# Layer norms of a decoder layer without statistics instructions: row sums from the residual adds, squares summed by ScalarE

## The chip, the cores and the metric

The kernel runs on one core of one Trainium2 chip. The metric is the device time of one execution in microseconds (us), from launch to end. Three executions of the kernel before took 700.11, 701.52 and 701.88 us; the median is 701.52 us. A further execution was recorded by the hardware profiler; all rows below come from that one.

Engines: PE is TensorE (matmul; PEld its weight loads), DVE is VectorE, ACT is ScalarE, POOL is GpSimd, SP is the engine whose queue issues most DMAs. Each engine runs its own list of instructions strictly in order and waits on semaphores (`s_...`) that others raise.

## What is computed

A decoder layer over 512 tokens of width 1024: a projection, sparse attention and an mLSTM, an output projection, then two layer norms around a mixture of experts, and a gated per-layer embedding. The change touches the two layer norms only.

```
def _layer_norm(x, g, b):
    mu = jnp.mean(xf, axis=-1, keepdims=True)
    var = jnp.mean(jnp.square(xf - mu), axis=-1, keepdims=True)
    y = (xf - mu) * lax.rsqrt(var + LN_EPS)
    return (y * g + b)

    ...
    mix = jnp.concatenate([y_a, y_m], axis=-1) @ w_out
    x = _layer_norm(DEEPNORM_ALPHA * x + mix, ln1_g, ln1_b)
    ffn = _hierarchical_moe(x, rg_w, rg_b, re_w, re_b, e_gate, e_up, e_down)
    x = _layer_norm(DEEPNORM_ALPHA * x + ffn, ln2_g, ln2_b)
    return x + jax.nn.sigmoid(x @ ple_gate_w) * (p_i @ ple_proj_w)
```

## The kernel before

Tokens stand on the 128 partitions in four tiles t = 0 to 3 of 128 tokens by 1024 features; the tile being normed is `mine[:, t, :]` (the buffer `res`). All order is written out by hand, one list per engine. Every large matmul product is taken in three passes on a high and a low part of each operand (`three`, L1693 to L1695); ACT rounds the high part, DVE subtracts it to give the low part.

**First norm, ahead of the router.** PE multiplies out the output projection per tile and half (`token_major`). When a half is done (`s_wot`), DVE's `mixed` adds it to the scaled residual (`residual`, L1346), then reads the half again with a statistics instruction (`norm_stats`, L1350); after the second half it merges the statistics (L1356), adds epsilon (L1358), and raises `s_ve`. POOL takes the power -0.5 (`inverse`, L698, `s_rs`). Meanwhile DVE subtracts the mean and multiplies by the norm's weights in place (`norm_centre`, L1362) and then, once POOL is done, scales and adds the bias (`norm_scale`, L1369, `s_ln`). PE turns the tile (`turn_first`, L1922: eight 128x128 transposes), ACT copies the two halves as high parts (L941), DVE makes the low parts (`low_first`, L1375). `route(0)` multiplies tiles 0 and 1 with the router's weights, `route(1)` tiles 2 and 3. Everything after (choice of experts, gather, experts) waits for `route(1)`.

**Second norm, behind the experts.** For each tile DVE adds the two experts' rows, each times its gate, to the residual (`expert_sum`, L1654, twice 128x1024), takes the statistics (`expert_variance`: L1350 twice, L1356, L1358), centres and scales. PE turns the tile, ACT and DVE make high and low parts (L1002, L1375), and PE multiplies with the gate's weights (`gate`, four quarters of 12 matmuls per tile and half). Ahead of that PE works off five products of the per-layer embedding (`embed`, L1933), and ACT carries each from PSUM to SBUF (`ple_out`, L936). In ACT's list all five `ple_out` stand ahead of the first copy of a turned tile:

```
            for u in range(AHEAD, 2 * NT):
                ple_out(u)
            act.wait_ge(s_glo, 2)
            ...
            for t in range(NT):
                turned_high(2 * t)
                turned_high(2 * t + 1)
```

In PE's list too, the five `embed` stand ahead of the first turn. Between the turns of tiles 0 and 1, ACT also rounds the last quarter of the gate's weights (`round_gate(3)`, L972), and DVE splits it (`split_gate(3)`, L1614) before PE's `gate(0, 3)`.

The code around the change:

Of the kernel before, what the change touches and what calls it, by code (L numbers as in the profile page):

```python
# [6 lines left out]
BF16 = mybir.dt.bfloat16  # L7
I32 = mybir.dt.int32
ALU = mybir.AluOpType
ACT = mybir.ActivationFunctionType  # L10
# [4 lines left out]
SEQ, DM = 512, 1024  # L15
# [6 lines left out]
EPS = 1e-5  # L22
# [51 lines left out]
def hybrid_layer(nc, d, out, x1_dram, pair_dram):  # L74
    ctx = ExitStack()
    with ctx:
# [3 lines left out]
        def sem(name):  # L80
            return ctx.enter_context(nc.semaphore(name))
# [188 lines left out]
        stat8 = small[:, 0:48].rearrange("p (t c) -> p t c", t=NT)  # L270
        mv8 = small[:, 48:56].rearrange("p (t c) -> p t c", t=NT)
        rs8 = small[:, 56:60]
        ve8 = small[:, 60:64]
        gate_w = [small[:, 64:68], small[:, 68:72]]
# [62 lines left out]

        s_pair = [sem(f"s_pair{t}") for t in range(NT)]
        s_ghi, s_glo, s_gt = sem("s_ghi"), sem("s_glo"), sem("s_gt")
        s_r2, s_bn2, s_ve2, s_rs2, s_ln2 = [sem(n) for n in ("s_r2", "s_bn2", "s_ve2", "s_rs2", "s_ln2")]  # L340
        s_x2t, s_x2hi, s_x2lo = sem("s_x2t"), sem("s_x2hi"), sem("s_x2lo")
        s_sig, s_mix, s_out = sem("s_sig"), sem("s_mix"), sem("s_out")
# [406 lines left out]
        def _(act):  # L749
# [184 lines left out]
            def ple_out(u):  # L934
                act.wait_ge(s_pp, u + 1)
                a.activation(ple_parts[u], ple_bank[u][:, :], ACT.Copy).then_inc(s_pev, 1)  # L936

            for u in range(2 * NT):
                t, half = u // 2, u % 2
                act.wait_ge(s_x1t, u + 1)  # L940
                a.activation(a_hi[:, 4 * half:4 * half + 4, t * P:(t + 1) * P],  # L941
                             turned_1[u][:, :].rearrange("p (k c) -> p k c", k=4), ACT.Copy).then_inc(s_x1hi, 1)
                if u == 1:
                    act.wait_ge(s_wr, 16)
                    act.wait_ge(s_wo, 2)
                    a.activation(w_hi[:, WR_AT:3 * GW], wr_raw.rearrange("p k c -> p (k c)"), ACT.Copy)\
                        .then_inc(s_wrs, 1)
                if u == 5:
                    copy_logits(0)
            copy_logits(1)  # L950

# [72 lines left out]
        def _(dve):  # L1024
# [319 lines left out]
            def residual(t, half):  # L1344
                r = mine[:, t, half * 512:(half + 1) * 512]
                v.scalar_tensor_tensor(out=r, in0=r, scalar=ALPHA, in1=bank[4 * (1 - half) + t][:, :],  # L1346
                                       op0=ALU.mult, op1=ALU.add).then_inc(s_r, 1)

            def norm_stats(t, half, count):
                v.bn_stats(stat8[:, t, 6 * half:6 * half + 6], mine[:, t, half * 512:(half + 1) * 512])\  # L1350
                    .then_inc(count, 1)

            def norm_variance(t, count, base, done):

                dve.wait_ge(count, base)
                v.bn_aggr(mv8[:, t, :], stat8[:, t, :]).then_inc(count, 1)  # L1356
                dve.wait_ge(count, base + 1)
                v.tensor_scalar(ve8[:, t:t + 1], mv8[:, t, 1:2], EPS, None, ALU.add).then_inc(done, 1)  # L1358

            def norm_centre(t, done):  # L1360
                m = mine[:, t, :]
                v.scalar_tensor_tensor(out=m, in0=m, scalar=mv8[:, t, 0:1], in1=ln_g, op0=ALU.subtract,  # L1362
                                       op1=ALU.mult).then_inc(done, 1)

            def norm_scale(t, done, ready):
                m = mine[:, t, :]
                dve.wait_ge(done, 2 * t + 1)
                dve.wait_ge(ready, t + 1)
                v.scalar_tensor_tensor(out=m, in0=m, scalar=rs8[:, t:t + 1], in1=ln_b, op0=ALU.mult,  # L1369
                                       op1=ALU.add).then_inc(done, 1)  # L1370

            def turned_low(u, banks, hi, lo):
# [7 lines left out]
            def mixed(t, half):  # L1380
                dve.wait_ge(s_xn[t], 16)
                dve.wait_ge(s_wot, 2 * t + half + 1)
                residual(t, half)
                dve.wait_ge(s_r, 2 * t + half + 1)
                norm_stats(t, half, s_bn)
                if half:
                    norm_variance(t, s_bn, 3 * t + 2, s_ve)
# [12 lines left out]
            mixed(1, 1)  # L1400
            norm_centre(1, s_ln)
            norm_scale(1, s_ln, s_rs)
            low_first(0)
            dve.wait_ge(s_wrs, 1)
            v.tensor_tensor(w_lo[:, WR_AT:3 * GW], wr_raw.rearrange("p k c -> p (k c)"),
                            w_hi[:, WR_AT:3 * GW].bitcast(F32), ALU.subtract).then_inc(s_wrs, 1)
            mixed(2, 0)
            mixed(2, 1)
            norm_centre(2, s_ln)
            mixed(3, 0)  # L1410
            norm_scale(2, s_ln, s_rs)
            low_first(1)
            mixed(3, 1)
            norm_centre(3, s_ln)
            norm_scale(3, s_ln, s_rs)
            low_first(2)
            low_first(3)

            n = [0]
# [228 lines left out]
            def expert_sum(t, k):  # L1648
                if k == 0:
                    dve.wait_ge(s_pair[t], 16)  # L1650
                else:
                    dve.wait_ge(s_xn[t], 32)
                dve.wait_ge(s_r2, NT + 2 * t + k)
                v.scalar_tensor_tensor(out=mine[:, t, :], in0=pair_of(t)[:, k, :], scalar=gate_w[k][:, t:t + 1],  # L1654
                                       in1=mine[:, t, :], op0=ALU.mult, op1=ALU.add).then_inc(s_r2, 1)

            def expert_variance(t):
                dve.wait_ge(s_r2, NT + 2 * t + 2)
                for half in range(2):
                    norm_stats(t, half, s_bn2)  # L1660
                norm_variance(t, s_bn2, 3 * t + 2, s_ve2)


            for t in range(NT):
                expert_sum(t, 0)
                if t:
                    turned_low(2 * t - 2, turned_2, s_x2hi, s_x2lo)
                    turned_low(2 * t - 1, turned_2, s_x2hi, s_x2lo)
                expert_sum(t, 1)
                expert_variance(t)  # L1670
                if t == 0:
                    dve.wait_ge(s_lnw2, 32)
                norm_centre(t, s_ln2)
                norm_scale(t, s_ln2, s_rs2)
# [503 lines left out]
```

## Time and profile before

| | us |
|---|---|
| median of three executions | 701.52 (700.11 to 701.88) |
| the profiled execution, whole | 696.23 |
| its span, first to last instruction | 694.4 |
| mean granted TensorE clock over the span | 0.964 of full speed |
| PE busy | 640.6 (92%) |
| DVE busy | 366.9 (53%) |
| ACT busy | 179.0 (26%) |
| POOL busy | 162.4 (23%) |

A row of a timeline reads: start in us from the span's start, duration in us, engine, line of the code, operation, what it writes and reads with shapes, how many such, and in brackets how long the engine had stood idle before and what ended the wait. Line numbers are those of the kernel before; in the changed kernel the same functions stand some 10 lines further down.

### The profile page before, as it was taken

Reading aid. Unit: us, or ns where it says so; the run is one execution under the profiler, and the core shown is the slowest. Engines: PE = TensorE matmul, PEld = TensorE weight load, DVE = VectorE, ACT = ScalarE, POOL = GpSimd, SP = SyncE. Lnnn points to the kernel's source line nnn. Section 1 sums busy time; section 2 is a strip of 40 time slices with the busy share of each in tenths; the row PEclk is TensorE's granted clock in tenths of the full one; section 3 lists DMA queues with packets and bytes.
Section 4 is the critical chain, followed back from the end, with each engine's and each line's share of the span. In section 5 each row is a group of like instructions: output and inputs, shape, how many; then the busy total and the mean of one; then the engine's idle time right before and its main releaser. Section 6 shows DMA issues by size and latency. Waiting matters only on the chain.

```text
span 694.4 us, 10082 instructions
## 1 busy us (share of the span) xinstructions
PE 640.6 (92%) x3766; PEld 445.2 (64%) x3766; DVE 366.9 (53%) x849; ACT 179.0 (26%) x344; POOL 162.4 (23%) x173
## 2 busy tenths in 40 slices
PE   4989999999989999899957999899999999897997
PEld 3758797777767778788734555555555555543785
DVE  3379999677675648675964223122221122118956
ACT  5265224324322423340211111111111111115321
POOL 7305615001010000041203233233333323211100
PEclk9959999999999999999997999999999999998999
DMA  6502401401400040119986899999999999987003
GB/s 237 207 0 66 179 0 31 181 1 41 142 0 1 3 179 1 33 62 369 387 340 221 298 404 418 416 416 415 413 417 414 414 414 414 407 325 280 41 0 122
DMA packets 30502, 151.21 MB, mean 218 GB/s; under 512 B 7372, under 2 KB 7628, under 8 KB 16496
## 3 DMA queue, kind: packets, MB, share of 16 engines
q1 hardware_dynamic: 24048, 142.08, 51.7%
q0 software_dynamic: 6400, 8.42, 3.4%
q8 instruction: 32, 0.52, 0.3%
q14 instruction: 22, 0.18, 0.1%
HBM read 148.36 MB, written 14.68 MB: 235 GB/s over the span
## 4 chain that ended last, share of the span: by engine, by line
PE 62%; DVE 8%; DMA 7%; issue 3%; SPq 2%; ACT 1%; POOL 1%; DVEq 0%; POOLq 0%; ACTq 0%
PE bank L2012 16%; PE bank L2027 9%; PE bank L1693 8%; PE bank L1694 8%; PE bank L1695 8%; DMA slots<-in_w_exp_dram 4%; PE bank L1773 3%; SPq L488 2%; PE bank L2002 2%; PE bank L1782 2%; PE bank L1794 1%; PE bank L1823 1%; PE bank L2019 1%; PE bank L1814 1%; POOL small L698 1%
## 5 line engine op out<-in xcount | busy, mean ns | idle before, releaser
L1605 DVE COPY rows_x<-bank 128x128 f32<-128x128 f32 x40 | 11.7, 292 | 186.0 <-issue 100.7
L1693 PE MATMUL bank<-w_hi,a_hi 128*128 128x384 f32 (+1 forms) x240 | 89.7, 374 | 3.9 <-POOL w_lo L629 2.9
L1694 PE MATMUL bank<-w_lo,a_hi 128*128 128x384 f32 (+1 forms) x240 | 87.6, 365 | 0.0
L1695 PE MATMUL bank<-w_hi,a_lo 128*128 128x384 f32 (+1 forms) x240 | 87.6, 365 | 0.0
L1693 PE MATMUL bank<-a_hi,w_hi 128*128 128x512 f32 (+1 forms) x176 | 70.9, 403 | 11.5 <-POOL w_lo L622 9.9
L713 POOL DMA_INDIRECT pair_dram<-rows_x,row_put x40 | 40.6, 1016 | 160.2 <-ACT rows_x L968 160.2
L2012 PE MATMUL bank<-raw,rows_x 128*64 128x256 f32 x640 | 73.5, 382 | 1.3 <-DVE rows_x L1579 0.8
L1694 PE MATMUL bank<-a_lo,w_hi 128*128 128x512 f32 (+1 forms) x176 | 69.3, 394 | 0.0
L1695 PE MATMUL bank<-a_hi,w_lo 128*128 128x512 f32 (+1 forms) x176 | 69.2, 393 | 0.0
L2012 PEld LDWEIGHTS bank<-raw,rows_x 128*64 128x64 f32 x640 | 46.8, 138 | 32.1 <-issue 11.1
L1693 PEld LDWEIGHTS bank<-w_hi,a_hi 128*128 128x128 f32 x240 | 46.1, 192 | 10.7 <-issue 2.7
L707 POOL DMA_INDIRECT y<-x_dram,row_got x40 | 41.3, 1032 | 37.5 <-DVE row_put L1540 23.6
L1694 PEld LDWEIGHTS bank<-w_lo,a_hi 128*128 128x128 f32 x240 | 46.1, 192 | 4.3
L968 ACT ACTIVATE rows_x<-bank 128x512 f32<-128x512 f32 x40 | 23.9, 598 | 96.6 <-PE bank L2027 96.6
L1695 PEld LDWEIGHTS bank<-w_hi,a_lo 128*128 128x128 f32 x240 | 45.9, 191 | 4.4
L1693 PEld LDWEIGHTS bank<-a_hi,w_hi 128*128 128x128 f32 (+1 forms) x176 | 33.5, 190 | 19.6 <-POOL w_lo L622 9.9
L2012 PE MATMUL bank<-slots,rows_x 128*64 128x256 f32 x384 | 43.8, 379 | 0.5 <-DMA slots<-in_w_exp_dram 0.5
L963 ACT ACTIVATE pa<-bank 128x128 f32<-128x128 f32 x40 | 11.1, 278 | 121.3 <-PE bank L2012 114.4
L2027 PE MATMUL bank<-raw,rows_x 128*64 128x512 f32 x160 | 38.7, 604 | 3.4 <-issue 2.6
L2012 PEld LDWEIGHTS bank<-slots,rows_x 128*64 128x64 f32 x384 | 28.9, 137 | 18.4 <-issue 6.7
L1695 PEld LDWEIGHTS bank<-a_hi,w_lo 128*128 128x128 f32 (+1 forms) x176 | 33.3, 189 | 7.1
L1694 PEld LDWEIGHTS bank<-a_lo,w_hi 128*128 128x128 f32 (+1 forms) x176 | 33.6, 191 | 6.5
(257 smaller groups left out, 1016.5 us busy)
## 6 DMA issues: line engine op xcount, KB each, us to landing
raw<-in_w_exp_dram SPq DMA_DIRECT2D x48, 1024.0 KB
slots<-in_w_exp_dram SPq DMA_DIRECT2D x27, 1024.0 KB
rows_x<-in_w_exp_dram SPq DMA_DIRECT2D x14, 1024.0 KB
raw<-in_w_in_dram SPq DMA_DIRECT2D x19, 512.0 KB, 3.7
y<-in_w_exp_dram SPq DMA_DIRECT2D x7, 1024.0 KB
raw<-in_w_wide_dram SPq DMA_DIRECT2D x4, 1536.0 KB, 6.7
raw<-in_w_out_dram SPq DMA_DIRECT2D x4, 1024.0 KB, 4.8
raw<-pair_dram SPq DMA_DIRECT2D x8, 512.0 KB, 6.3
```

The lines of the kernel that those rows point to most:

```text
L488: sp.dma_start(pieces[s][q], src).then_inc(s_ew[s][q], 16)
L707: g.indirect_dma_start(out=x_got[s], out_offset=None, in_=x1_halves, in_offset=bass.IndirectOffsetOnAxis(ap=row_got[:, c:c + 1], axis=0), ...
L713: g.indirect_dma_start(out=pair_halves, out_offset=bass.IndirectOffsetOnAxis(ap=row_put[:, c:c + 1], axis=0), in_=y_out[s], in_offset=None ...
L968: a.activation(y_out[s], bank[4 + s % 2][:, :], ACT.Copy).then_inc(s_outa, 1)
L1693: t_.matmul(o, lh, rh, start=first, stop=False)
L1694: t_.matmul(o, lh, rl, start=False, stop=False)
L1695: return t_.matmul(o, ll, rh, start=False, stop=last)
L1773: t_.matmul(score_bank[U % 2][:, 0:(b + 1) * P], q_t[rows, g % 2, b * P:(b + 1) * P], k_t[rows, g % 2, 0:(b + 1) * P], start=True, stop=Tr ...
L1782: mm = t_.transpose(turn_bank[:, s * P:(s + 1) * P], prob[:, U % 2, s * P:(s + 1) * P], ident[:, :])
L2002: mm = t_.transpose(bank[2 + s % 2][:, c * P:(c + 1) * P], x_got[s][:, c * P:(c + 1) * P], ident[:, :])
L2012: mm = t_.matmul(gu_bank[par][f * SEATS:(f + 1) * SEATS, 0:2 * P], xt[par][:, at_:at_ + SEATS], expert_rows(s, q)[:, c, f * 2 * P:(f + 1) ...
L2027: mm = t_.matmul(bank[4 + par][half * SEATS:(half + 1) * SEATS, :], ht[:, f * SEATS:(f + 1) * SEATS], expert_rows(s, 2)[:, 2 * half + f, : ...
```

## The change

The statistics instructions go. Each operation that leaves the sum to be normed in `mine` also leaves the sum of its row (`accum_out`); one small DVE operation (`norm_mean`) makes minus the mean of it and raises `s_bn` (`s_bn2` in the second norm). ACT then squares the whole tile with that as bias and sums the squares (`square`, raises `s_sq` or `s_sq2`); a small DVE operation turns the sum into variance plus epsilon. `norm_centre` writes to a place of its own, since ACT still reads `mine`; `norm_scale` reads it there. In the first norm DVE's list is in another order too. POOL's, PE's and SP's lists stay as they are.

```
-            def norm_stats(t, half, count):
-                v.bn_stats(stat8[:, t, 6 * half:6 * half + 6], mine[:, t, half * 512:(half + 1) * 512])\
...
+                                       op0=ALU.mult, op1=ALU.add, accum_out=row_sum[half][:, t:t + 1]).then_inc(s_r, 1)
...
+            def norm_mean(t, second, done):
+                v.tensor_scalar(neg_mean[:, t:t + 1], row_sum[0][:, t:t + 1], second, -1.0 / DM, ALU.add,
+                                ALU.mult).then_inc(done, 1)
...
+            def norm_centre(t, centred, mean, done):
+                dve.wait_ge(mean, t + 1)
+                v.scalar_tensor_tensor(out=centred, in0=mine[:, t, :], scalar=neg_mean[:, t:t + 1], in1=ln_g, op0=ALU.add,
                                        op1=ALU.mult).then_inc(done, 1)
...
+            def norm_variance(t, squares, done):
+                dve.wait_ge(squares, t + 1)
+                v.tensor_scalar(ve8[:, t:t + 1], square_sum[:, t:t + 1], 1.0 / DM, EPS, ALU.mult, ALU.add)\
...
+            dve.wait_ge(s_lnw, 32)
             mixed(0, 0)
             mixed(0, 1)
-            dve.wait_ge(s_lnw, 32)
-            norm_centre(0, s_ln)
-            norm_scale(0, s_ln, s_rs)
             mixed(1, 0)
+            norm_scale(0, centred_1, s_ln, s_rs)
             mixed(1, 1)
...
```

ACT's side of it, first norm and second norm:

```
+            def square(t, mean, squares, done):
+                act.wait_ge(mean, t + 1)
+                a.activation(squares, mine[:, t, :], ACT.Square, bias=neg_mean[:, t:t + 1],
+                             accum_out=square_sum[:, t:t + 1]).then_inc(done, 1)
...
+            square(0, s_bn, squares_1, s_sq)
+            act.wait_ge(s_wr, 16)
+            act.wait_ge(s_wo, 2)
+            a.activation(w_hi[:, WR_AT:3 * GW], wr_raw.rearrange("p k c -> p (k c)"), ACT.Copy).then_inc(s_wrs, 1)
+            square(1, s_bn, squares_1, s_sq)
             for u in range(2 * NT):
                 t, half = u // 2, u % 2
+                if u == 2:
+                    square(2, s_bn, squares_1, s_sq)
...
                 if u == 5:
+                    square(3, s_bn, squares_1, s_sq)
                     copy_logits(0)
...
             for t in range(NT):
+                if t == 0:
+                    square(0, s_bn2, squares_2, s_sq2)
                 turned_high(2 * t)
                 turned_high(2 * t + 1)
+                if t + 1 < NT:
+                    square(t + 1, s_bn2, squares_2, s_sq2)
```

What stands in ACT's list behind the experts, before. The `raw<-bank` rows are the five `ple_out`, `a_hi<-bank` the copies of turned tiles, `last_hi` is `round_gate(3)`:

```order
L968 ACTIVATE rows_x<-bank 128x512 [waits s_put3,s_dn]
L409 REGISTER_ALU
L409 COMPARE_AND_BRANCH
L408 UNCONDITIONAL_BRANCH
L936 ACTIVATE raw<-bank 128x512 [waits s_pp] x5
L1002 ACTIVATE a_hi<-bank 128x4x128 [waits s_x2t,s_glo]
L1002 ACTIVATE a_hi<-bank 128x4x128 [waits s_x2t]
L972 ACTIVATE last_hi<-y 128x2048 [waits s_quarter3]
```

And now, where `raw,small<-res,small` is the new `square`:

```order
L979 ACTIVATE rows_x<-bank 128x512 [waits s_put3,s_dn]
L412 REGISTER_ALU
L412 COMPARE_AND_BRANCH
L411 UNCONDITIONAL_BRANCH
L939 ACTIVATE raw<-bank 128x512 [waits s_pp] x5
L943 ACTIVATE raw,small<-res,small 128x1024 [waits s_bn2,s_glo]
L1013 ACTIVATE a_hi<-bank 128x4x128 [waits s_x2t] x2
L943 ACTIVATE raw,small<-res,small 128x1024 [waits s_bn2]
L983 ACTIVATE last_hi<-y 128x2048 [waits s_quarter3]
```

The square of tile 0 stands behind the five `ple_out`, that of tile 1 ahead of `round_gate(3)`.

DVE's list at the same place, before: the two expert sums of tile 0, its norm, and the first sum of tile 1.

```order
L1654 SCALAR_TENSOR_TENSOR res<-raw,small,res 128x1024 [waits s_r2,s_xn0]
L1350 BN_STATS small<-res 128x6 [waits s_r2]
L1350 BN_STATS small<-res 128x6
L1356 BN_AGGR small<-small 128x2 [waits s_bn2]
L1358 TENSOR_SCALAR small<-small 128x1 [waits s_bn2]
L1362 SCALAR_TENSOR_TENSOR res<-res,small,pa 128x1024 [waits s_lnw2]
L1369 SCALAR_TENSOR_TENSOR res<-res,small,pa 128x1024 [waits s_rs2,s_ln2]
L1654 SCALAR_TENSOR_TENSOR res<-raw,small,res 128x1024 [waits s_r2,s_pair1]
```

And now:

```order
L1665 SCALAR_TENSOR_TENSOR res,small<-raw,small,res 128x1024 [waits s_r2,s_xn0]
L1367 TENSOR_SCALAR small<-small 128x1 [waits s_r2,s_lnw2]
L1372 SCALAR_TENSOR_TENSOR raw<-res,small,pa 128x1024 [waits s_bn2]
L1377 TENSOR_SCALAR small<-small 128x1 [waits s_sq2]
L1383 SCALAR_TENSOR_TENSOR res<-raw,small,pa 128x1024 [waits s_rs2,s_ln2]
L1665 SCALAR_TENSOR_TENSOR res,small<-raw,small,res 128x1024 [waits s_r2,s_pair1]
```

The centring moved ahead of the variance, and the variance (L1377) waits for ACT's `s_sq2` where before it waited for DVE's own statistics. Behind it in the list stand the scaling and all work on tile 1.

DVE's list in the first norm now, from the second half of tile 2 to the last low parts:

```order
L1361 SCALAR_TENSOR_TENSOR res,small<-res,bank 128x512 [waits s_wot,s_xn3]
L1383 SCALAR_TENSOR_TENSOR res<-pa,small 128x1024 [waits s_rs,s_ln]
L1389 TENSOR_TENSOR a_lo<-bank,a_hi 128x4x128 [waits s_x1hi] x2
L1361 SCALAR_TENSOR_TENSOR res,small<-res,bank 128x512 [waits s_wot,s_xn3]
L1367 TENSOR_SCALAR small<-small 128x1 [waits s_r]
L1372 SCALAR_TENSOR_TENSOR pa<-res,small,pa 128x1024 [waits s_bn]
L1377 TENSOR_SCALAR small<-small 128x1 [waits s_sq]
L1389 TENSOR_TENSOR a_lo<-bank,a_hi 128x4x128 [waits s_x1hi] x2
L1383 SCALAR_TENSOR_TENSOR res<-pa,small 128x1024 [waits s_rs,s_ln]
L1389 TENSOR_TENSOR a_lo<-bank,a_hi 128x4x128 [waits s_x1hi] x2
```

The low parts of tile 2 stand ahead of the last scaling, where before they stood behind it.

## Rows read from the trace of the kernel before

**Rows 1.** Chain of waits in order of time, second norm, tile 0: start, us, what.
```profile
634.68 1.30 DVE res L1654
636.00 1.30 DVE small L1350 x2
...
637.81 1.55 POOL small L698
```
**Rows 2.** Timeline of ACT behind the experts.
```profile
640.75 0.60 ACT L936 ACTIVATE raw<-bank 128x512 f32<-128x512 f32 x1 [1.12 <-PE bank L1933]
641.60 1.08 ACT L1002 ACTIVATE a_hi<-bank 128x512 fp32r<-128x512 f32 x2 [0.25 <-PE bank L1922]
645.29 1.92 ACT L972 ACTIVATE last_hi<-y 128x2048 fp32r<-128x2048 f32 x1 [2.60 <-DMA y<-in_ple_gate_dram]
```
**Rows 3.** Timeline of PE behind the experts, to the first matmul of the gate.
```profile
629.27 11.44 PE L1933 MATMUL bank<-pa 128*128 128x512 f32 x20 [5.07 <-issue]
640.88 1.06 PE L1922 MATMUL bank<-ident,res 128*128 128x128 f32 x8 [0.17 <-DVE res L1369]
642.98 0.50 PE L1693 MATMUL bank<-w_hi,a_hi 128*128 128x512 f32 x1 [1.04 <-DVE a_lo L1375]
```
**Rows 4.** Windows: length, busy (count) of PE, PEld, DVE, ACT, POOL, clock, DMA.
```profile
624.50:629.20 4.70, 0.00 (x0) 0.00 (x0) 2.52 (x2) 4.70 (x4) 0.98 (x1) 0.84 0.19 72
629.30:634.30 5.00, 5.00 (x6) 2.16 (x7) 5.00 (x3) 1.54 (x2) 0.00 (x0) 0.50 0.83 301
634.80:640.70 5.90, 5.90 (x14) 2.28 (x12) 5.26 (x8) 1.79 (x3) 1.54 (x1) 1.00 1.00 379
643.00:690.00 47.00, 46.85 (x216) 38.41 (x216) 33.90 (x45) 10.56 (x16) 4.55 (x3) 1.00 0.13 48
351.40:354.60 3.20, 3.20 (x17) 2.71 (x16) 0.00 (x0) 0.00 (x0) 0.00 (x0) 0.50 1.02 420
```
**Rows 5.** Groups of DVE instructions by line and shape: count, busy us, mean ns.
```profile
L1350 DVE BATCH_NORM_STATS2 small<-res 128x6 f32<-128x512 f32 x16 | 10.7, 690 | 0.4
L1654 DVE SCALAR_TENSOR_TENSOR res<-raw,small,res 128x1024 f32<-128x1024 f32 x8 | 10.2, 1278 | 0.1
L1362 DVE SCALAR_TENSOR_TENSOR res<-res,small,pa 128x1024 f32<-128x1024 f32 x8 | 10.2, 1276 | 0.0
L1358 DVE TENSOR_SCALAR small<-small 128x1 f32<-128x1 f32 x8 | 1.2, 154 | 0.3
```
**Rows 6.** Groups of ACT, then of DVE: operations that leave a sum, reads of it.
```profile
L822 ACT ACTIVATION_READ_ACCUMULATOR raw<-raw,small 128x1 f32 x32 | 6.0, 187 | 0.0
L822 ACT ACTIVATE raw<-raw,small 128x512 f32<-128x512 f32 x8 | 5.8, 723 | 4.7 <-DVE small L1143 4.7
...
L822 ACT ACTIVATE raw<-raw,small 128x128 f32<-128x128 f32 x8 | 3.2, 402 | 10.7 <-DVE small L1143 10.6
...
L1138 DVE DVE_READ_ACCUMULATOR2_ANT small<- 128x1 f32 x32 | 2.7, 83 | 0.0
```
**Rows 7.** Timeline of DVE in the first norm, tiles 0, 1 and 3.
```profile
322.86 1.28 DVE L1362 SCALAR_TENSOR_TENSOR res<-res,small,pa 128x1024 f32<-128x1024 f32 x1
...
326.54 0.69 DVE L1346 SCALAR_TENSOR_TENSOR res<-res,bank 128x512 f32<-128x512 f32 x1 [0.60 <-PE bank L1695]
...
329.26 0.69 DVE L1346 SCALAR_TENSOR_TENSOR res<-res,bank 128x512 f32<-128x512 f32 x1 [1.30 <-PE bank L1695]
...
343.57 0.68 DVE L1346 SCALAR_TENSOR_TENSOR res<-res,bank 128x512 f32<-128x512 f32 x1
...
347.12 1.28 DVE L1369 SCALAR_TENSOR_TENSOR res<-res,small,pa 128x1024 f32<-128x1024 f32 x1 [0.52 <-POOL small L698]
```
**Rows 8.** Timeline of PE in the first norm: turns of tiles 2 and 3, second router half.
```profile
342.51 1.09 PE L1922 MATMUL bank<-ident,res 128*128 128x128 f32 x8 [0.69 <-DVE res L1369]
...
348.46 1.09 PE L1922 MATMUL bank<-ident,res 128*128 128x128 f32 x8 [1.70 <-DVE res L1369]
...
351.13 0.39 PE L1693 MATMUL bank<-a_hi,w_hi 128*36 128x256 f32 x1 [1.33 <-DVE a_lo L1375]
```

More of the change, by code:

```diff
@@ L1346, in residual, with norm_scale @@
                 v.scalar_tensor_tensor(out=r, in0=r, scalar=ALPHA, in1=bank[4 * (1 - half) + t][:, :],
-                                       op0=ALU.mult, op1=ALU.add).then_inc(s_r, 1)
-            def norm_stats(t, half, count):
-                v.bn_stats(stat8[:, t, 6 * half:6 * half + 6], mine[:, t, half * 512:(half + 1) * 512])\
[L1351 to L1362, printed above, removed]
-                                       op1=ALU.mult).then_inc(done, 1)
-            def norm_scale(t, done, ready):
-                m = mine[:, t, :]
+                                       op0=ALU.mult, op1=ALU.add, accum_out=row_sum[half][:, t:t + 1]).then_inc(s_r, 1)
[5 more added lines that the diff above has]
+                v.scalar_tensor_tensor(out=centred, in0=mine[:, t, :], scalar=neg_mean[:, t:t + 1], in1=ln_g, op0=ALU.add,
+                                       op1=ALU.mult).then_inc(done, 1)
+            def norm_variance(t, squares, done):
+                dve.wait_ge(squares, t + 1)
+                v.tensor_scalar(ve8[:, t:t + 1], square_sum[:, t:t + 1], 1.0 / DM, EPS, ALU.mult, ALU.add)\
+                    .then_inc(done, 1)
+            def norm_scale(t, centred, done, ready):
                 dve.wait_ge(done, 2 * t + 1)
                 dve.wait_ge(ready, t + 1)
-                v.scalar_tensor_tensor(out=m, in0=m, scalar=rs8[:, t:t + 1], in1=ln_b, op0=ALU.mult,
+                v.scalar_tensor_tensor(out=mine[:, t, :], in0=centred, scalar=rs8[:, t:t + 1], in1=ln_b, op0=ALU.mult,
                                        op1=ALU.add).then_inc(done, 1)
@@ L1383, in mixed @@
                 residual(t, half)
-                dve.wait_ge(s_r, 2 * t + half + 1)
-                norm_stats(t, half, s_bn)
                 if half:
-                    norm_variance(t, s_bn, 3 * t + 2, s_ve)
+                    dve.wait_ge(s_r, 2 * t + 2)
+                    norm_mean(t, row_sum[1][:, t:t + 1], s_bn)
+                    norm_centre(t, centred_1, s_bn, s_ln)
+                    norm_variance(t, s_sq, s_ve)
             def low_first(t):
@@ L1654, in expert_sum @@
                 v.scalar_tensor_tensor(out=mine[:, t, :], in0=pair_of(t)[:, k, :], scalar=gate_w[k][:, t:t + 1],
[L1655 to L1661, printed above, removed]
+                                       in1=mine[:, t, :], op0=ALU.mult, op1=ALU.add,
+                                       accum_out=row_sum[0][:, t:t + 1]).then_inc(s_r2, 1)
             for t in range(NT):
@@ L1669, in _ @@
                 expert_sum(t, 1)
-                expert_variance(t)
                 if t == 0:
                     dve.wait_ge(s_lnw2, 32)
-                norm_centre(t, s_ln2)
-                norm_scale(t, s_ln2, s_rs2)
+                dve.wait_ge(s_r2, NT + 2 * t + 2)
+                norm_mean(t, 0.0, s_bn2)
+                norm_centre(t, centred_2, s_bn2, s_ln2)
+                norm_variance(t, s_sq2, s_ve2)
+                norm_scale(t, centred_2, s_ln2, s_rs2)
                 if t == 1:
```

22 lines of the change are left out of this document (8 added, 14 removed).

## The prediction, written before the changed kernel ran

> **What bounds the kernel now.** I read the page first: PE is busy 92% of the span, so DVE instructions that are saved count only where PE waits. I then looked for PE's waits next to the two norms in its timeline, and followed the chain of waits there.
>
> Behind the experts, the chain of waits runs through DVE: the second expert sum of tile 0 (634.68), the statistics (636.00), POOL's power (637.81) [rows 1], the scaling, and the turn of tile 0 at 640.88. But PE's timeline shows that the turn could not have started much earlier: PE works on the five embedding products from 629.27 until 640.71, and has stood idle for 0.17 us when the turn starts [rows 3]. So two chains end together there, and DVE's is the later by 0.17 us. From 642.98 on PE has the gate's products: in the window from 643 to 690 it is busy 46.85 of 47.00 us [rows 4]. Whatever comes late before 642.98 is not made up later.
>
> ACT's timeline: the last of the five copies of embedding products starts at 640.75, released by PE, and takes 0.60; the copy of the turned tile follows at 641.60 [rows 2]. ACT has no slack in which it could do something earlier for tile 0, unless this stands in its list ahead of that copy.
>
> In the first norm, PE waits for DVE before the turn of tile 2 (0.69 us), before that of tile 3 (1.70) and before the second router half (1.33) [rows 8]. This chain decides when the experts start.
>
> **Second norm, tile 0.** This is where the sum is made. In the changed list of ACT the square of tile 0 stands behind the five copies; in that of DVE the variance of tile 0 waits for the square, and behind it stand the scaling and all of tile 1. DVE has the mean ready soon: the second sum ends at 635.98, and `norm_mean` costs 0.15 [rows 5], so 636.2. ACT takes the square up when the last copy is done, at 640.75 + 0.60 = 641.3 [rows 2]. That is 5.1 us of waiting that the list makes, not the data.
>
> Duration of the square. No row shows this operation. Nearest are ACT operations with a pointer bias and a sum: 402 ns at 128 elements, 723 ns at 512, so 0.836 ns an element and 723 + 428 = 1151 ns at 1024. A read of the accumulator (187 ns) follows, starting some 0.09 before the end [rows 6]. From start to sum: 1.25 us. Bounds: 1.15 if the read hides, 1.34 if it doesn't overlap.
>
> From there: 641.3 + 1.25 = 642.55; hand-over 0.05, variance 0.15 [rows 5]: 642.75; hand-over 0.08, power 1.53: 644.35; hand-over 0.1, scaling 1.28: 645.75. Before, the power began at 637.81 and ended at 639.36 [rows 1], and the turn started at 640.88; the end of the scaling before is therefore about 640.7. **Tile 0 is turned 5.0 us later**, at 645.9 instead of 640.88. The statistics that are dropped there (two of 690 ns, an aggregate) save nothing: they lie in the time in which DVE now waits for ACT. PE has nothing else in its list to fill the gap, so it stands idle from 640.7 to 645.9.
>
> **What PE's idle time does to its clock.** After an idle stretch of 4.7 us (624.5 to 629.2, with the clock at a mean of 0.84 as it falls) the next 5.0 us run at 0.50, which is 1.2 GHz: 6 embedding matmuls in 5.0 us. Then it is 1.00, 2.4 GHz: 14 in 5.9 us [rows 4]. Work at the low level takes twice as long. The new idle stretch is 5.2 us, as long as that one. If the clock again stays low for 5.0 us after work resumes at 645.9, that is until 650.9: the turn, its copies and the low part take 2.1 us from turn to gate (640.88 to 642.98 [rows 3]) plus 0.3 for the transposes, and the gate's first 2.6 us run at half rate, which costs 1.3. Together 1.6. Bounds: 0 if the clock doesn't fall, 2.8 if the whole low stretch of 5.0 us falls on the gate. The other low stretch at hand (351.4 to 354.6) is 3.2 us long [rows 4] and would cost 0.7. I take 1.6, since the idle time ahead of it is the same as in the longer one.
>
> **Second norm, tiles 1 to 3.** PE needs 47/4 = 11.9 us a tile [rows 4]. DVE's chain of a tile: two sums 2.56, low parts 1.3, mean 0.2, square 1.3 (the centring of 1.28 runs beside it), variance 0.2, power 1.7, scaling 1.28: 8.5. That fits. The tightest point is the last quarter of the gate's weights: the square of tile 1 stands ahead of its rounding (1.92 [rows 2]) on ACT. DVE is through with the scaling of tile 1 at about 645.7 + 8.5 = 654.3 and splits the quarter until 656.6; PE asks for it after three quarters of tile 0 and the turn, at 648.0 + 8.2 + 1.0 = 657.2 at full clock, later at the low one. Cost: nothing, with 0.6 us to spare.
>
> **First norm.** Here squares stand well in ACT's list: ACT is idle where they come. DVE now waits for both norm weights before its first sum. Before, the same wait stood ahead of the centring at 322.86 and cost no idle time. So it is over by then; sums, mean and centring of tile 0 take 2.9 us more, up to 325.8, and the next sum can't start before PE releases it at 326.54 [rows 7]. Cost: nothing.
>
> Tile 1: its second sum starts at 329.26, released by PE, as before [rows 7]. From the start of such a sum to the scaling is now: 0.74 for the sum with its read of the accumulator (a read takes 83 ns [rows 6]), mean 0.15, square 1.25, variance 0.15, power 1.53, and 0.28 in hand-overs: 4.1 us. Before it was 3.55 (343.57 to 347.12 [rows 7]). The scaling of tile 1 starts 0.5 later, at 333.4. From there to the second sum of tile 3 DVE had 10.7 us; it loses three statistics (2.1), an aggregate (0.25) and the split of the router's weights, moved into the wait before (0.4), gains a mean (0.2) and a wait of about 1.2 for POOL: 9.4. So the second sum of tile 3 starts at about 342.8, 0.8 earlier, and its scaling at 342.8 + 4.1 = 346.9, 0.2 earlier than 347.12. What DVE gained in work, it gives back in the longer way through ACT. The low parts of tile 2 no longer stand between this scaling and those of tile 3, but the latter wait for ACT's copies anyway. I take **-0.1 us** for the router's start, with bounds of -0.8 (hand-overs free, short square) and +0.6 (a sum with accumulator costs 0.1 more, five times over). The low clock in the second router half stays [rows 4]; PE is idle a little longer before it, not less.
>
> The experts themselves are untouched and move with their start.
>
> **Sum.** +5.0 (square behind the copies) + 1.6 (clock) - 0.1 (first norm) = **+6.5 us**. Against the profiled execution: 696.23 + 6.5 = 702.7, with a span of 700.9. The three timed executions have a median of 701.52, 5.3 more than the profiled one; the change applies to them alike: 708.0.
>
> **A rule that speaks against the change.** The expert sum reads two fp32 tensors in SBUF and takes 1278 ns for 1024 elements, 1.25 ns an element; the centring with as many takes 1276 [rows 5]. With a sum left besides, no row shows it. The Trainium skill, "Vector Engine (DVE) Microarchitecture Reference", section "Points that are easy to get wrong", says that such an instruction with two non-bf16 SBUF sources runs at half throughput, since no port is left for the accumulator. By that rule the sum above would grow by half a microsecond to two; the rows without an accumulator don't show a halving. What it would be as a mechanism is the first rival.
>
> **Rivals.**
> 1. *The expert sums take twice as long once they leave a sum* (2.56 instead of 1.28). For tile 0 this hides: the mean is ready at 638.7, still before 641.3. For tile 1 the two sums push the split of the last quarter from 656.6 to 659.2, while PE asks at 657.2 plus the low clock's 1.6, so 0.4 to 2 late; tiles 2 and 3 need 8.5 + 2.6 = 11.1, under 11.9. Time: 708.4 to 710. Against it: a custom operation with a sum keeps its pace, with an 83 ns read [rows 6].
> 2. *The clock doesn't fall* in the new gap, or falls only for a short stretch: 706.3 to 707. For it: in the first norm idle stretches of 1 to 2 us leave PE at full clock in part. Against: the gap is over 5 us.
> 3. *Other side, no change*: in the timed executions the experts' rows land later against the embedding products than in the profiled one; their time is 5.3 us longer, and I can't see where. The price of the square's place is 641.3 minus the time of the mean (636.2 plus the lateness). From 5.1 us of lateness on it is zero. Then the way from sum to scaling counts, 3.4 now against 3.47 before: 701.4. Against it: rows and embedding products both hang on the end of the experts.
> 4. *Faster*: as 3, and the 0.8 us that DVE gains in the first norm reach the router so that PE's idle time and with it the low stretch before the experts go (1.6 us): 699. It needs the square of tile 0 to start by about 637.5; the list rules that out unless 3 holds.
>
> **Chances.** Forecast as summed 0.70, rival 1 0.05, rival 2 0.14, rival 3 0.07, rival 4 0.04. The forecast's own range is 706.5 to 709.5; the range for 8 in 10 takes in rivals 1 and 2, a router half whose low stretch shrinks, and the spread of the timed executions: 704.5 to 710.8. About 0.3% (2 us) is what a measurement of this kernel can tell from no change. Faster by more 0.04, within it 0.07, slower by more 0.89.
>
> **What would show it.** In the profile after: ACT's square of tile 0 of the second norm directly behind the fifth copy, while DVE stands idle some 5 us ahead of its variance, released by ACT; the turn of tile 0 5 us behind the end of PE's embedding products; granted clock 0.50 at the start of the gate. In the first norm: PE's turn of tile 2 about 0.7 us earlier, that of tile 3 nearly where it was. The prediction is wrong if the variance of tile 0 is ready before 640, if the gate starts within 1 us of where it did, or if PE keeps its full clock through the gap.

## The result, and the profile after

The changed kernel takes 703.75 us (median of 22 runs, 699.98 to 707.91), the kernel before 699.75 us (22 runs, 696.09 to 703.17). The ratio is 1.0057, 95% interval 1.0040 to 1.0073: **slower by 4.0 us**. Forecast were +6.5 us and 708.0. The direction held, the size did not, and 703.75 lies below the range. The three runs shown at first (median 701.52) lay 1.8 us above the median of all 22, which makes up part of the miss; the other 2.5 us are an error of the sum.

The profiled execution takes 701.4 us, its span is 699.6 (before: 696.23 and 694.4), the mean granted clock 0.962 (0.964).

**The last tile's way, second norm.** The chain of waits of the changed kernel behind the experts; it answers to [rows 1]. Start, us, what.

```profile
632.33 7.36 PE bank L1941 x16
...
639.71 0.02 ACT raw L939
...
640.21 1.24 ACT raw L943 x2
...
641.47 0.16 DVE small L1377
...
641.71 0.58 POOL small L701
...
642.38 1.29 DVE res L1383
...
643.81 1.10 PE bank L1930 x4
```

The chain has left DVE: it comes out of PE's embedding products through ACT's last copy (L939) into the square (L943), then variance, power, scaling, turn. DVE's timeline at the same place (start, us, operation, idle time before it and what ended it):

```profile
634.20 1.28 DVE L1665 SCALAR_TENSOR_TENSOR res<-raw,small,res 128x1024 f32<-128x1024 f32 x1
635.41 0.08 DVE L1665 DVE_READ_ACCUMULATOR res<-raw,small,res 128x1 f32 x1
635.61 0.15 DVE L1367 TENSOR_SCALAR small<-small 128x1 f32<-128x1 f32 x1
635.80 1.28 DVE L1372 SCALAR_TENSOR_TENSOR raw<-res,small,pa 128x1024 f32<-128x1024 f32 x1
641.47 0.15 DVE L1377 TENSOR_SCALAR small<-small 128x1 f32<-128x1 f32 x1 [4.39 <-ACT raw L943]
642.38 1.28 DVE L1383 SCALAR_TENSOR_TENSOR res<-raw,small,pa 128x1024 f32<-128x1024 f32 x1 [0.76 <-POOL small L701]
```

The mean is ready at 635.76, the square starts at 640.21: 4.45 us are the place in ACT's list. The expert sum with an accumulator still takes 1.28 us, plus 0.08 for the read. PE's timeline answers to [rows 3]; the last line is the gate's last matmul.

```profile
628.55 11.12 PE L1941 MATMUL bank<-pa 128*128 128x512 f32 x20 [5.35 <-issue]
643.81 1.94 PE L1930 MATMUL bank<-ident,res 128*128 128x128 f32 x8 [4.13 <-DVE res L1383]
646.31 0.80 PE L1701 MATMUL bank<-w_hi,a_hi 128*128 128x512 f32 x1 [0.56 <-DVE a_lo L1389]
...
694.62 0.40 PE L1703 MATMUL bank<-last_hi,a_lo 128*128 128x512 f32 x1
```

In these windows, as in [rows 4], the seventh column is the granted clock. The last line is the second router half, in the first norm.

```profile
640.00:642.00 2.00, 0.00 (x0) 0.00 (x0) 0.15 (x1) 1.44 (x3) 0.29 (x1) 1.00 1.04 434
642.00:644.00 2.00, 0.19 (x1) 0.22 (x2) 1.62 (x2) 0.00 (x0) 0.28 (x1) 0.85 0.52 217
...
646.00:648.00 2.00, 1.69 (x4) 1.41 (x5) 1.84 (x3) 0.38 (x1) 0.00 (x0) 0.50 0.00 0
648.00:650.00 2.00, 2.00 (x6) 1.52 (x6) 1.89 (x5) 1.47 (x3) 0.00 (x0) 0.50 0.00 0
650.00:652.00 2.00, 2.00 (x10) 1.63 (x9) 1.31 (x2) 1.58 (x1) 0.55 (x1) 0.94 0.00 0
...
351.40:354.30 2.90, 2.87 (x24) 2.59 (x24) 0.00 (x0) 0.00 (x0) 0.00 (x0) 1.00 1.05 439
```

The clock is still full in PE's gap and falls near its end; the gate's first 3.8 us (646.3 to about 650.1) run at half rate, 6 matmuls in 2 us instead of 10 or 11. The router half, at 0.50 before [rows 4], now has 1.00.

POOL's powers (the rows of `inverse`, the power -0.5), tile 3 of the first norm and tile 0 of the second:

```profile
346.40 0.54 POOL L701 TENSOR_TENSOR small<-small 128x1 f32<-128x1 f32 x1 [6.16 <-DVE small L1377]
...
641.71 0.57 POOL L701 TENSOR_TENSOR small<-small 128x1 f32<-128x1 f32 x1 [16.11 <-DVE small L1377]
```

Before, the same operation took 1.55 us in the chain [rows 1]. That is the part that I had not foreseen. PE in the first norm, against [rows 8]:

```profile
343.29 1.04 PE L1930 MATMUL bank<-ident,res 128*128 128x128 f32 x8
...
348.77 1.09 PE L1930 MATMUL bank<-ident,res 128*128 128x128 f32 x8 [1.65 <-DVE res L1383]
...
351.44 0.31 PE L1701 MATMUL bank<-a_hi,w_hi 128*36 128x256 f32 x1 [1.33 <-DVE a_lo L1389]
```

The 0.69 us of idle time before the turn of tile 2 are gone. DVE's second sum of tile 3 and the scaling of that tile:

```profile
343.56 0.69 DVE L1361 SCALAR_TENSOR_TENSOR res<-res,bank 128x512 f32<-128x512 f32 x1 [0.53 <-PE bank L1703]
...
347.44 1.28 DVE L1383 SCALAR_TENSOR_TENSOR res<-pa,small 128x1024 f32<-128x1024 f32 x1
```

DVE waits for PE there; before, the same sum followed DVE's own work without a wait [rows 7].

**Where the time went.** The profiled execution of after is 5.2 us longer than that of before. Its stretches, after minus before, from the starts and ends of rows:

| stretch | us |
|---|---|
| start to the second sum of tile 1, first norm (329.26 to 330.87) | +1.61 |
| from there to the second router half (351.13 to 351.44) | -1.30 |
| second router half, start to ACT's copy of it (4.55 to 2.97) | -1.58 |
| to the end of the embedding products (640.71; now 639.68) | +0.24 |
| end of products to turn (0.17 to 4.13) | +3.96 |
| turn to gate (2.10 to 2.50) | +0.40 |
| gate to the start of its last matmul | +1.83 |

I take the first line as spread between executions: the first experiment below, the same program up to the second norm, starts its second router half 2.40 us earlier in its profile (349.04). The rest sums to +3.55, against 4.0 timed (2.8 to 5.1 by the interval).

### The profile page after: what moved, and what is told of

Its sections match the earlier page's. It is cut to its first block, busy times and chain, and to the rows that moved or that the text cites. A ratio compares the mean times of both kernels' runs of the same rounds, so it can differ in the third digit from the quotient of the medians.

```text
span 699.6 us, 10099 instructions
## 1 busy us (share of the span) xinstructions
PE 641.8 (92%) x3766; PEld 447.2 (64%) x3766; DVE 357.4 (51%) x849; ACT 188.5 (27%) x360; POOL 154.1 (22%) x173
## 4 chain that ended last, share of the span: by engine, by line
PE 65%; DVE 7%; DMA 5%; issue 3%; ACT 1%; POOL 0%; DVEq 0%; ACTq 0%; SPq 0%; POOLq 0%
PE bank L2020 18%; PE bank L2035 9%; PE bank L1701 8%; PE bank L1703 8%; PE bank L1702 8%; DMA slots<-in_w_exp_dram 4%; PE bank L1781 2%; PE bank L2010 2%; PE bank L1941 2%; PE bank L1790 2%; PE bank L1802 1%; PE bank L2027 1%; PE bank L1831 1%; PE bank L1822 1%; PE bank L1930 1%
```

## The experiments

All are compared with the kernel before; the ratio is that of medians. Three theories come in them. **P**: the square's place in ACT's list makes the gap. **S**: POOL's power takes 1.5 us when it is issued while DVE executes a centring, because this reads two tensors in SBUF, and 0.55 otherwise; before, the centring (L1362: `mine` and `ln_g`, both in SBUF) started just ahead of each power. **C**: the gap also lowers PE's clock, and the gate pays for it.

**1. The square behind the second of five copies.**

```
 for u in range(AHEAD, 2 * NT):
     ple_out(u)
+    if u == 4:
+        square(0, s_bn2, squares_2, s_sq2)
...
-                if t == 0:
-                    square(0, s_bn2, squares_2, s_sq2)
```

> The changed kernel with one edit: ACT's square of tile 0 of the second norm stands behind the second of the five copies of embedding products instead of behind the fifth. Theory P (place in ACT's list): DVE's wait ahead of the variance of tile 0 falls from 4.4 us to under 1.5; tile 0 is turned within 0.3 us of the end of PE's embedding products (639.7 in the changed kernel's trace), not 4.1 behind it; the clock stays full through the gate's start; from the end of the embedding products to the last matmul of the gate 49 us instead of 55.3. Against the kernel before: what the first norm gives, -1.3 us or more, so a ratio of 0.995 to 0.999. Rival L (the longer way through ACT and back costs by itself, wherever the square stands): the tail stays over 52 us and the ratio stays above 1.003.

Measured: 697.16 us, ratio 0.9965 (0.9939 to 0.9991), span 690.1. ACT and PE:

```profile
632.61 1.15 ACT L943 ACTIVATE raw<-res,small 128x1024 bf16<-128x1024 f32 x1 [0.31 <-DVE small L1367]
```

```profile
625.32 11.49 PE L1941 MATMUL bank<-pa 128*128 128x512 f32 x20 [5.46 <-issue]
636.65 1.04 PE L1930 MATMUL bank<-ident,res 128*128 128x128 f32 x8
638.72 0.50 PE L1701 MATMUL bank<-w_hi,a_hi 128*128 128x512 f32 x1 [1.03 <-DVE a_lo L1389]
```

The square now waits for the mean (0.31 us, ended by DVE) and no longer for the list; the turn follows the products without idle time, and the clock stays 1.00. The three copies that are left are hidden. Against the changed kernel that is 0.92% or 6.4 us; in the two profiles it is 48.5 us from the end of the products to the start of the last matmul (636.65 to 685.18), against 54.9 (639.68 to 694.62). P holds. This version is faster than both kernels.

**2 and 3. One norm alone.** The second kernel has the change in the first norm and the old statistics in the second (the expert sum leaves no sum there, and ACT has no squares); the third the other way round.

```
 # 2: second norm
-                norm_mean(t, 0.0, s_bn2)
-                norm_centre(t, centred_2, s_bn2, s_ln2)
-                norm_variance(t, s_sq2, s_ve2)
-                norm_scale(t, centred_2, s_ln2, s_rs2)
+                for half in range(2):
+                    old_stats(t, half, s_bn2)
+                old_variance(t, s_bn2, 3 * t + 2, s_ve2)
...
+                old_centre(t, s_ln2)
+                old_scale(t, s_ln2, s_rs2)
```

> The first norm as in the changed kernel, the second as before. If the first norm alone gives 1.3 us through DVE (as the two traces show between the second sum of tile 1 and the second router half), the ratio is 0.996 to 0.999; with the low clock stretch in the second router half also gone in every run, 0.995 or less. By my prediction (-0.1 us) it would be 1.000. The power on POOL is expected at 0.54 us in the first norm and 1.52 in the second.

> The first norm as before, the second as in the changed kernel. If the loss sits in the second norm alone: DVE's wait for ACT 4.4 us ahead of the variance of tile 0, tail from the end of the embedding products to the last gate matmul 55 us against 49, ratio 1.007 to 1.010 (6.2 us of 700 is 1.0089). If the first norm gave nothing in timed runs, this ratio would be that of the whole change, 1.0057. The power 1.52 us in the first norm, 0.55 in the second.

Measured: first norm only 698.45, ratio 0.9979 (0.9960 to 0.9998); second only 703.68, ratio 1.0069 (1.0045 to 1.0093). The two add up to +0.48%; the whole change has +0.57%. So the first norm alone is a gain of some 1.5 us (interval 0.1 to 2.8), where I had forecast 0.1, and the loss is all in the second (4.8 us). The profiles put both higher: in the table the first norm gives 1.30 + 1.58 = 2.9 us and the second costs 6.2. How many of the timed executions have the low router half before, I can't tell. In each profile the power takes 0.55 where the norm is new and 1.52 where it is old, and the second router half runs at full clock with the new first norm only.

**4. The centring behind the variance**, in both norms. The same instructions; only the order of two changes.

```
-                norm_centre(t, centred_2, s_bn2, s_ln2)
                 norm_variance(t, s_sq2, s_ve2)
+                norm_centre(t, centred_2, s_bn2, s_ln2)
```

> The changed kernel with DVE's centring behind the variance instead of ahead of it, in both norms, so that it runs beside POOL's power again, as in the kernel before. Theory S (a DVE operation that reads two SBUF tensors holds POOL up): the power is recorded at 1.4 to 1.6 us instead of 0.54 and ends some 0.4 behind the centring; tile 0 of the second norm is scaled 1.0 to 1.2 us later than in the changed kernel. Rival V (the power is shorter because its operand or its place differs): it stays at 0.54 and the scaling comes 0.5 to 0.6 later, when the centring ends. Time: by S 1 us from the tail and up to 1 us from the first norm, ratio to before 1.007 to 1.010.

Measured: 706.49 (6 runs), ratio 1.0113 (1.0081 to 1.0146), above the 1.007 to 1.010 expected; the router half is at the low clock again here (0.60). DVE's timeline, then POOL's:

```profile
643.98 0.15 DVE L1377 TENSOR_SCALAR small<-small 128x1 f32<-128x1 f32 x1 [5.06 <-ACT raw L943]
644.05 1.27 DVE L1372 SCALAR_TENSOR_TENSOR raw<-res,small,pa 128x1024 f32<-128x1024 f32 x1
645.86 1.28 DVE L1383 SCALAR_TENSOR_TENSOR res<-raw,small,pa 128x1024 f32<-128x1024 f32 x1 [0.53 <-POOL small L701]
```

```profile
644.22 1.54 POOL L701 TENSOR_TENSOR small<-small 128x1 f32<-128x1 f32 x1 [15.32 <-DVE small L1377]
```

The power is issued at 644.22, 0.17 us into the centring, and ends at 645.76, 0.44 after the centring's end (645.32). All eight powers take 1.51 to 1.54. Now take a DVE operation that has one source in PSUM: in the changed kernel the low parts of tile 2 (L1389, `bank` and `a_hi`) run from 346.24 for 1.28 us, and the power at 346.40 takes 0.54 beside them. So it is not that DVE is busy. Nor is it the kind of operation: the split of the router's weights (L1416) is a `TENSOR_TENSOR` like those low parts, but both its sources, `y` and `w_hi`, are in SBUF. In the changed kernel:

```profile
333.20 0.45 DVE L1416 TENSOR_TENSOR w_lo<-y,w_hi 128x288 fp32r<-128x288 f32 x1
```

```profile
333.36 0.70 POOL L701 TENSOR_TENSOR small<-small 128x1 f32<-128x1 f32 x1 [7.28 <-DVE small L1377]
```

The power ends 0.41 us behind the end of the split (334.06 and 333.65), as it ends 0.44 behind that of the centring. S holds: it is where DVE's sources lie. In time, the held-up power is only a part: of the 0.97 us by which the idle time before the turn grew (5.10 against 4.13), DVE waits 0.53 for POOL behind the centring; the rest is the centring itself, which no longer runs beside ACT's square. The Trainium skill, "SBUF — State Buffer", section "SBUF: two separate sides", says it so: a DVE operation with two SBUF inputs and a GpSimd operation that reads SBUF need the same pair of ports, and whichever starts first has it until it ends. The trace agrees (1.54 against 0.54), and by that rule the prediction would have had the power at its short value, since the diff takes the centring away from beside it.

**5. PE kept busy in the gap.** Eight extra fp32 products of 512 columns ahead of the turn of tile 0, into a bank that nothing else uses then. Their result goes nowhere.

```
+                    if t == 0:
+                        for i in range(8):
+                            t_.matmul(bank[2][:, :], p_raw[:, 0, 0:P], proj_raw[:, 0:512], start=i == 0, stop=i == 7)
                     pe.wait_ge(s_ln2, 2 * t + 2)
```

> The changed kernel with eight more matmuls of PE (512 columns, into a bank that is free) between the last embedding product and the turn of tile 0 of the second norm, 3.4 us of work in a gap of 4.1; their result is overwritten and read by nobody. Theory C (of the loss in the second norm, 2.2 us are the low clock after the gap: 0.4 in turn and copies, 1.8 in the gate): the clock stays at 1.00, from the start of the turn to the last gate matmul 49.0 us instead of 51.2, the turn itself where it was, ratio to before 1.001 to 1.004. Rival N: the gate is slow for another reason (weights landing late, a bank not free), the extra work changes nothing and the ratio stays at 1.005 to 1.007.

Measured: 704.75, ratio 1.0075 (1.0051 to 1.0100). I had mis-sized the extra work: it took 7.03 us, each product being two passes in the profile, and pushed the turn itself back. In the time this run therefore decides nothing. The profile shows more: the clock stays at 1.00 and from the turn to the start of the last matmul it is 48.5 us, against 50.8 in the changed kernel.

**6. The square behind the fourth copy** (`u == 6` in the edit of 1).

> As the kernel with the early square, but the square of tile 0 stands behind the fourth of the five copies. If the lateness is set by the end of the copy ahead of it and nothing else, ACT takes it up 1.7 us earlier than in the changed kernel and the turn comes 2.4 us after the end of the embedding products (4.1 there, 0 with the square behind the second). Clock: in the changed kernel the level fell 3.7 us into the gap; with a gap of 2.4 us it should still be full at the turn. If it holds through the gate, the tail is 51.5 us and the ratio to before 1.000 to 1.002; if it falls after the turn, 1 to 2 us more.

Measured: 701.69, ratio 1.0038 (1.0017 to 1.0060), between experiment 1 and the changed kernel, though the intervals of these two ratios, 1.0057 and 1.0038, overlap. PE's timeline and windows:

```profile
641.78 1.06 PE L1930 MATMUL bank<-ident,res 128*128 128x128 f32 x8 [2.42 <-DVE res L1383]
...
643.88 0.80 PE L1701 MATMUL bank<-w_hi,a_hi 128*128 128x512 f32 x1 [1.04 <-DVE a_lo L1389]
```

```profile
642.00:644.00 2.00, 0.96 (x9) 0.73 (x7) 1.70 (x4) 1.08 (x2) 0.00 (x0) 0.74 0.60 252
644.00:646.00 2.00, 2.00 (x5) 1.61 (x6) 1.93 (x5) 0.15 (x1) 0.00 (x0) 0.50 0.04 16
```

The idle time went from 4.13 to 2.42 us, one copy's distance (1.71) earlier: P again, now by size. But the low clock is not saved with it. The turn still runs at full clock (1.06 us for eight); the clock falls in PE's next wait, and the gate starts low.

**7. One embedding product later.** Experiment 1, and in addition the last of the five products stands between the turn of tile 0 and the gate, where PE waits for the low part (1.03 us above).

```
+                        if t == 0:
+                            embed(2 * NT - 1)
...
+                if t == 0:
+                    ple_out(2 * NT - 1)
```

The upper lines are PE's, behind the turn; the lower ones ACT's, behind `turned_high(1)`; both loops ahead end one earlier.

> The kernel with the early square, and the last embedding product moved from ahead of the turn of tile 0 to between the turn and the gate, with ACT's copy of it behind the copies of tile 0. Before, PE stood idle there for 1.03 us, and the turn was held up by the products alone. With the early square DVE is through with the scaling about 1 us ahead of the end of the products, so the turn can move up by up to 1.0 us and the product (1.7 us) covers the idle time: 1 us less than the early square alone, ratio to before 0.993 to 0.997. Rival: the copy of the product delays ACT's square of tile 1 and the rounding of the last quarter of the gate's weights, and nothing is won.

Measured: 696.12, ratio 0.9960 (0.9938 to 0.9982), span 692.4: not to be told from experiment 1. In its profile the product covers the wait between turn and gate (product at 639.41, gate at 640.72 at once), but PE now idles for 1.51 us ahead of the turn: with a product less before it, DVE's chain is the later. One wait was exchanged for another.

**8. Experiment 1 with the centring behind the variance in the first norm only.** It was meant to price S in the first norm.

> The kernel with the early square, with the centring behind the variance in the first norm only, so that POOL's power runs beside it there (1.52 us instead of 0.54). This prices the power in the first norm apart from the second. If the gain of the first norm hangs on POOL running undisturbed, the second router half starts 1 us later against the turn of tile 0 and its low clock stretch (1.6 us) may come back: ratio to before 0.999 to 1.001, against 0.9965 for the early square alone. If the gain came from the shorter work of DVE, it stays at 0.996 to 0.998.

Measured: 700.85, ratio 1.0025 (0.9997 to 1.0052), 0.6% or 4 us above experiment 1. PE's timeline:

```profile
350.88 1.97 PE L1930 MATMUL bank<-ident,res 128*128 128x128 f32 x8 [2.85 <-DVE res L1383]
...
354.26 0.43 PE L1701 MATMUL bank<-a_hi,w_hi 128*36 128x256 f32 x1 [1.05 <-DVE a_lo L1389]
```

The powers there take 1.51 to 1.52 again. But DVE hardly waits for them. Its timeline in tile 3, and POOL's:

```profile
347.08 0.15 DVE L1377 TENSOR_SCALAR small<-small 128x1 f32<-128x1 f32 x1 [1.31 <-ACT dist L943]
...
349.55 1.27 DVE L1383 SCALAR_TENSOR_TENSOR res<-pa,small 128x1024 f32<-128x1024 f32 x1
```

```profile
347.31 1.51 POOL L701 TENSOR_TENSOR small<-small 128x1 f32<-128x1 f32 x1 [5.00 <-DVE small L1377]
```

The power is done at 348.82, and the scaling starts 0.73 later, behind the centring and the low parts of tile 2; only in tile 1 does DVE wait for POOL, 0.16 us. What it waits for is ACT, 1.31 us ahead of each variance, since the centring no longer fills that time. So this run prices the place of the centring, and S next to nothing. From the second sum of tile 1 on, the turn of tile 3 comes 1.79 us later than in experiment 1 (19.69 and 17.90). Behind it come the low clock's 0.72 from the turn to the router half and 1.27 in the half itself: 3.8 us together, near the 4 timed and more than I had expected. In this profile the gate's start was at a low clock too (first matmul 0.79 us), with only 1.16 us of idle time ahead of its turn. Why the clock fell there and not in experiment 9 (0.61 us), I can't show.

**9. Four extra products instead of eight** (`range(4)`, `stop=i == 3`), which fit into the gap.

> The changed kernel with four extra fp32 products of 512 columns on PE between the last embedding product and the turn of tile 0, into a bank that the gate has not started on (extra work, no result uses it). The eight of the run before this one took 7.0 us, so these take 3.5 us, inside the 4.1 us for which PE waits for DVE's scaling. Theory C (the idle stretch lowers PE's clock and that costs the gate 2.2 us): the turn starts where it did, 4.1 us behind the end of the embedding products, the clock stays 1.00, turn to last matmul about 48.5 us instead of 50.8, time 0.997 to 0.998 of the changed kernel's, so 1.002 to 1.003 of the kernel before. Rival (the 2.2 us come from the gate's inputs being late, not from the clock): turn to last matmul stays 50.8, ratio 1.005 to 1.006.

Measured: 700.89, ratio 1.0028 (1.0000 to 1.0056). PE's timeline, then a window:

```profile
637.84 3.60 PE L2109 MATMUL bank<-pa 128*128 128x512 f32 x8
642.05 1.10 PE L1930 MATMUL bank<-ident,res 128*128 128x128 f32 x8 [0.61 <-DVE res L1383]
644.12 0.50 PE L1701 MATMUL bank<-w_hi,a_hi 128*128 128x512 f32 x1 [0.97 <-DVE a_lo L1389]
...
690.59 0.40 PE L1703 MATMUL bank<-last_hi,a_lo 128*128 128x512 f32 x1
```

```profile
644.00:646.00 2.00, 1.88 (x8) 1.58 (x9) 1.97 (x5) 0.00 (x0) 0.00 (x0) 1.00 0.00 0
```

The turn comes 4.0 us behind the end of the embedding products, as in the changed kernel; every input of the gate comes as late as there. What differs is the clock, 1.00 throughout, and from the turn to the last matmul it is 48.54 us (690.59 - 642.05) instead of 50.81. In the profiles C holds: 2.27 us of the tail are the clock. The time agrees, 0.29% below the changed kernel's ratio, but does not show it alone: the intervals overlap (1.0000 to 1.0056 and 1.0040 to 1.0073).

## Why the prediction was right in direction and wrong in size

- **The square's place: right.** The chain was the one forecast: copy, square, variance, power, scaling, turn, with DVE idle ahead of the variance (4.39 us). The square took 1.22 us from start to sum (640.21 to 641.43); 1.25 was forecast. Experiments 1 and 6 move the place and the gap with it.
- **The power behind it: wrong, and the first step that failed.** I took 1.53 us from the row before and kept it, as a property of the operation. It took 0.57: the rest of the 1.55 of [rows 1] was a wait for the centring beside it, which the change moves away. That is 1.0 of the 5.0 us; the gap grew by 3.96. Experiment 4 moves the centring back beside the power: 1.54 again, and 5.10 us of idle time before the turn, near the prediction's 5.2, which had the long power without the centring that causes it.
- **The clock: mechanism right, size too small.** I took 1.6 us, on a low stretch of 5.0 us from the turn on. It lasted some 6.3 (643.8 to 650.1) and cost 0.40 + 1.83 = 2.23; experiment 9 has 2.27.
- **The first norm: wrong by over a microsecond.** Forecast was -0.1: "what DVE gained in work, it gives back in the longer way through ACT". The stretch came out at -1.30. Two terms rest on the power's 1.53. The way of tile 1 from sum to scaling had 4.1 and took 3.30 (330.87 to 334.17), with a power of 0.70; and of the "wait of about 1.2 for POOL" there is nothing. So the second sum of tile 3 came 12.69 us behind that of tile 1 (14.31 before, 13.5 forecast), and PE, not DVE, set it: DVE waited 0.31 and 0.53 us for PE on the way. Tile 3's own way did get longer, 3.88 against 3.55 before (4.1 forecast), for the low parts of tile 2 now stand ahead of the scaling: the power is done at 346.94, they at 347.44. The signs of it: the turn of tile 2 came 0.83 us earlier against the second sum of tile 1, as forecast (0.7), that of tile 3 1.30 earlier, where it was to stay. Experiment 2 shows the gain of the first norm; how much of it is the freed power and how much the dropped statistics, no run separates.
- **"The low clock in the second router half stays": wrong**, and its reason, "PE is idle a little longer before it, not less", too. The half is at full clock in the changed kernel and in experiments 1, 2, 5, 6, 7 and 9, and low before and in 3, 4 and 8, the ones with the old order or the centring behind the variance. That is another -1.58 us. PE's waits from the turn of tile 2 on are 0.69, 0.20, 1.70 and 1.33 us before, and 1.65 and 1.33 in the changed kernel: the first two are gone. In experiments 4 and 8 the first of them is gone too, but the wait ahead of tile 3 is 2.87 and 2.85. Which of these waits decides was not taken apart.
- **The tiles behind: right.** Tiles 1 to 3 of the second norm are hidden, and the split of the last quarter (ended 654.17) came in time. The wait for both norm weights cost nothing, as said: DVE's first sum waited for them until 322.42, its centring ended at 325.29, and PE released the next sum at 328.15.
- **Rival 1 (expert sums twice as long): wrong.** 1.28 + 0.08 us. The rule of the Trainium skill named beside it ("Vector Engine (DVE) Microarchitecture Reference", "Points that are easy to get wrong"), half throughput for such an instruction with two non-bf16 SBUF sources, does not show here: 1.28 us with the sum and without it. Rival 2 fell with the clock of 0.50, rivals 3 and 4 with the chain.
- **The base.** Three runs gave 701.52; 22 gave 699.75. With the later base the forecast would have been 706.25, still 2.5 too high, and its range 702.7 to 709.0. That the measured time lies below the stated range takes both, the base and the terms above.

In sum: +5.0 + 1.6 - 0.1 = 6.5 was forecast; +3.96 + 2.23 - 1.30 - 1.58 = +3.3 is what those terms measured, with one term (-1.58) that was not in the sum. The loss was forecast for the right reason; two of its terms were mis-sized by a power whose length was a wait, one by the length of the low stretch, and one was put at nothing.

## What to carry to other kernels

When a dependence is moved to another engine, its price is what stands ahead in that engine's list at that moment; here a square of 1.2 us cost 4 us and, moved three copies up, nothing. The duration of a short GpSimd operation in a trace may be a wait: look at what DVE does in that time and whether both its sources are in SBUF, before carrying the number over to an order that changes this. Work that hides under a wait for another engine, as the centring under ACT's square, comes to light when it is moved behind the wait. And a gap on a bound PE is worth more than its length: here 4.1 us of idle time took 2.2 more from the work behind it.

## What the runs showed of the hardware

- A POOL `TENSOR_TENSOR` on 128x1 takes 0.54 to 0.57 us alone or beside a DVE operation with a PSUM source, 1.51 to 1.54 when it is issued just behind the start of a 1.28 us DVE operation with two SBUF sources, and 0.70 behind the start of a 0.45 us one (a split of 128x288). In the last two cases it ends 0.41 to 0.44 us behind the DVE operation.
- A DVE sum of two fp32 SBUF tensors of 128x1024 takes 1.28 us with an accumulator as without; the read adds 0.08. ACT's square of 128x1024 with bias and sum takes 1.15, and its sum is there 1.22 after the start.
- After 4.1 us of idle time PE's granted clock was 0.50, 1.2 GHz, for some 6.3 us; after 2.4 us (experiment 6) the turn still ran at full clock and the fall came 1.2 us behind its start, in the next wait. Extra products in the gap kept it at 1.00, 2.4 GHz.
